# Where the first weight piece of the next stage is loaded and split: eighth chunk or last chunk

## The reference

```python
def swiglu(x, w_gate, w_up, w_down):
    return (jax.nn.silu(x @ w_gate) * (x @ w_up)) @ w_down

# first block
n = modulate(rmsnorm(h, g_pre[l, 0]), shift(0), scale(0))
f = swiglu(n, w_ffn_gate[l, 0], w_ffn_up[l, 0], w_ffn_down[l, 0])
h = h + 0.5 * gate(0) * rmsnorm(f, g_post[l, 0])
...
# a mixer (two attentions) and a second swiglu follow; the second block is alike:
mod = c_act @ ada_w[l] + ada_b[l]
h = modulate_2(rms_norm(x, ffn1_norm[l]), sh1, sc1)
x = x + 0.5 * g1[:, None, :] * swiglu_2(h, ffn1_w_gate[l], ffn1_w_up[l], ffn1_w_down[l])
```

## Time and profile before

| | us |
|---|---|
| median of 3 runs | 1094.05 (1093.93 to 1094.06) |
| the profiled execution's own time | 1094.11 |
| its span | 1092.4 |
| PE busy | 1062.3 (97%) |
| DVE busy | 854.6 (78%) |
| ACT busy | 548.9 (50%) |
| granted TensorE clock | 0.999 |

### The profile page before, as it was taken

How to read it: one execution, slowest core, us unless ns; L and a number is a source line. 1 busy time by engine, 2 the same in 40 slices (tenths; PEclk the granted TensorE clock), 3 DMA queues, 4 the chain that set the end, 5 groups by cost and what they waited for, 6 DMA issues and landing times.

```text
span 1092.4 us, 16231 instructions
## 1 busy us (share of the span) xinstructions
PE 1062.3 (97%) x6159; PEld 927.3 (85%) x6159; DVE 854.6 (78%) x931; ACT 548.9 (50%) x664; POOL 50.3 (5%) x78
## 2 busy tenths in 40 slices
PE   3999999999999999999999999999999999999997
PEld 2999999889988788888978888898887778888886
DVE  6899888678887788887778988877876787666665
ACT  4444343564765654444564444454654456444452
POOL 1000000011121100000010000000100000000001
PEclk9999999999999999999999999999999999999999
DMA  9999997546424599997569999844562536767651
GB/s 342 381 400 391 388 394 261 178 118 221 148 78 154 178 337 312 325 316 234 203 232 343 344 367 342 281 167 135 179 209 100 192 117 212 234 216 233 218 176 58
DMA packets 147141, 265.26 MB, mean 243 GB/s; under 512 B 9770, under 2 KB 104471, under 8 KB 141975
## 3 DMA queue, kind: packets, MB, share of 16 engines
q1 hardware_dynamic: 145376, 261.30, 69.4%
q0 software_dynamic: 1056, 3.17, 0.8%
q10 hardware_dynamic: 662, 0.16, 0.1%
HBM read 263.34 MB, written 1.27 MB: 242 GB/s over the span
## 4 chain that ended last, share of the span: by engine, by line
PE 87%; DVE 4%; DMA 3%; ACT 2%; issue 2%; SPq 1%; POOL 1%; POOLq 0%; DVEq 0%; ACTq 0%
PE ps L1957 18%; PE ps L1888 12%; PE ps L1889 11%; PE ps L1890 11%; PE ps L1963 9%; PE ps L1938 6%; PE ps L1941 6%; PE ps L1940 6%; DMA w_raw<-in_w_ffn_up 1%; ACT w_hi L824 1%; DMA arena<-in_w_ada 1%; DVE w_lo L1209 1%; DVE y_row L1370 1%; PE ps L1908 1%; PE ps L2432 1%
## 5 line engine op out<-in xcount | busy, mean ns | idle before, releaser
L1209 DVE TENSOR_TENSOR w_lo<-w_raw,w_hi 128x2048 fp32r<-128x2048 f32 (+2 forms) x169 | 380.7, 2255 | 104.8 <-ACT w_hi L824 103.8
L824 ACT ACTIVATE w_hi<-w_raw 128x2048 fp32r<-128x2048 f32 (+2 forms) x169 | 317.5, 1883 | 248.8 <-PE ps L1890 93.7
L1957 PE MATMUL ps<-nT_both,w_hi 128*128 128x512 f32 x864 | 210.8, 391 | 0.0
L1957 PEld LDWEIGHTS ps<-nT_both,w_hi 128*128 128x128 f32 x864 | 158.6, 188 | 31.0
L1938 PE MATMUL ps<-nT_both,w_hi 128*128 128x256 f32 x576 | 164.3, 285 | 0.0
L1940 PE MATMUL ps<-nT_both,w_hi 128*128 128x256 f32 x576 | 162.9, 283 | 0.0
L1941 PE MATMUL ps<-nT_both,w_lo 128*128 128x256 f32 x576 | 162.9, 283 | 0.0
L1291 DVE SCALAR_TENSOR_TENSOR arena<-arena,c_act 128x3072 f32<-128x3072 f32 (+2 forms) x49 | 129.4, 2650 | 0.5 <-DMA arena<-in_ada_w 0.5
L1888 PE MATMUL ps<-w_hi,hT_hi 128*128 128x512 f32 x320 | 125.0, 391 | 0.0
L1889 PE MATMUL ps<-w_lo,hT_hi 128*128 128x512 f32 x320 | 125.0, 391 | 0.0
L1890 PE MATMUL ps<-w_hi,hT_lo 128*128 128x512 f32 x320 | 124.5, 389 | 0.0
(11 more groups left out here) (296 smaller groups left out, 1217.7 us busy)
## 6 DMA issues: line engine op xcount, KB each, us to landing
arena<-in_w_ada SPq DMA_DIRECT2D x16, 1536.0 KB, 9.2
arena<-in_ada_w SPq DMA_DIRECT2D x16, 1536.0 KB, 8.5
w_raw<-in_w_in SPq DMA_DIRECT2D x44, 512.0 KB, 4.6
w_raw<-in_ffn_w_down SPq DMA_DIRECT2D x44, 512.0 KB, 4.1
w_raw<-in_w_ffn_gate SPq DMA_DIRECT2D x42, 512.0 KB, 6.7
w_raw<-in_w_ffn_up SPq DMA_DIRECT2D x42, 512.0 KB, 7.7
w_raw<-in_w_ffn_down SPq DMA_DIRECT2D x42, 512.0 KB, 4.6
w_raw<-in_ffn_w_gate SPq DMA_DIRECT2D x42, 512.0 KB, 4.1
```

The source lines that it names most:

```text
L824: copy = lambda o, i: act.activation(o, i, ACT.Copy)
L1209: dve.tensor_tensor(lo(s, n), raw(s, n), hi(s, n).bitcast(F32), ALU.subtract).then_inc(lo_ready[s], 1)
L1957: pe.matmul(ps[:, i, :], hi(s)[:, cols], nT_both[:, 4 * half + k].rearrange("p a n -> p (a n)"), start=(half == 0 and k == 0), stop=False, ...
```

## The change

In F1 and F2 the load of the next stage's E piece moves on SP from behind the down piece of chunk 9 to before `chunk(8)`, that is, behind the B piece of chunk 8 and ahead of the down piece of chunk 7. Its hi split on ACT and its lo split on DVE move from the body of chunk 10 to the body of chunk 8. The loops of the three engines end one chunk earlier, and chunk 8 is written out behind them. F0 and F3 are unchanged, and so is PE's program.

```diff
+        EARLY_NEXT = ("F1", "F2")
...
-                with sp.Fori(3 if f == "F0" else 2, KD + 1) as c:
+                with sp.Fori(3 if f == "F0" else 2, KD if f in EARLY_NEXT else KD + 1) as c:
                     chunk(c)
+                if f in EARLY_NEXT:
+                    next_e()
+                    chunk(KD)
                 load_down(f, NC - 3)
...
                 load_down(f, NC - 2)
-                next_e()
+                if f not in EARLY_NEXT:
+                    next_e()
                 load_down(f, NC - 1)
                 next_b()
...
-                with act.Fori(2, NC - 1) as c:
+                with act.Fori(2, KD if f in EARLY_NEXT else NC - 1) as c:
                     body(f, c)
-                body(f, NC - 1, extra=next_e and (*next_e, n))
+                if f in EARLY_NEXT:
+                    body(f, KD, extra=(*next_e, n))
+                    body(f, NC - 2)
+                body(f, NC - 1, extra=f not in EARLY_NEXT and next_e and (*next_e, n))
...
-                with dve.Fori(3 if f == "F0" else 2, KD + 1) as c:
+                with dve.Fori(3 if f == "F0" else 2, KD if f in EARLY_NEXT else KD + 1) as c:
                     body(f, c, mods=True)
+                if f in EARLY_NEXT:
+                    body(f, KD, mods=True, extra=next_e)
                 body(f, NC - 2, hook=lambda: fold_all(f))
-                body(f, NC - 1, hook=lambda: outs(f), extra=next_e)
+                body(f, NC - 1, hook=lambda: outs(f), extra=None if f in EARLY_NEXT else next_e)
```

## The result

The median is 1096.28 us over 16 runs (1095.54 to 1097.86), against 1094.22 us (1093.85 to 1094.92) for the kernel before in the same measurement. The ratio is 1.0019, with an interval of 1.0012 to 1.0026. The kernel is 2.06 us slower. The forecast was 1096.0 and 2.0 us slower, with a range of 1094.6 to 1097.3.

What follows compares the result with a forecast made beforehand. PE was taken as the bound, busy 1062.3 of 1092.4 us. Removal 0, F1 0 and F2 1.97 us summed to 2.0 us slower, 1096.0 us (ratio 1.0018), with a range of 1094.6 to 1097.3.

Steps and rivals of the forecast that it cites:

- Removal, 0: Last chunks of F1 and F2: taking E's splits out gains 0; bound of the gain is PE's gaps, 1.12 us.
- F1, 0: F1's chunk 8: the product moves by 2.21 us, still ends 0.47 us ahead of PE, so the cost is 0.
- F2, DVE's own share, 0.84: F2's chunk 8: DVE's 2.21 us split moves the product to 701.69, past PE's start at 700.85; PE waits 0.84 us.
- F2, the load's share, 0.98: F2's chunk 8: E's load delays ada half 0, DVE begins 0.98 us late, and all of it reaches the product.
- If ada half 0 lands on time: Sign of a wrong prediction, F2's chunk 8: DVE's ada half 0 was expected to wait about 1 us for its DMA.
- the push of 1.46: F2's chunk 8, DMA queue: the 0.57 MB of E that miss the gap push later loads back 1.46 us.
- the move out of the loop: Loops end a chunk earlier: register and branch work of a few tens of ns moves; cost 0, 0.3 us either way.
- Restart, 0.1: F2, behind PE's wait before chunk 9: 0.1 us, the difference between the 1.87 us wait and the 1.97 us sum.
- (a): Rival, F2's chunk 8: only DVE's work counts, 0.84 us, ada half 0 lands in time; 1094.9 us; chance 0.14.
- (b): Rival, F2's chunk 8: slower, the push is complete and ada half 0 is 2.7 us late; 1097.2 us; chance 0.15.
- (c): Rival: no wait or a small gain, PE's end gaps shrink and F2's reserve suffices; more likely 1094.0 us; chance 0.07.
- (d): Rival: the load waits in SP's queue for slot E, while the splits still move; time as DVE-only or worse; chance 0.02.

Runs made afterwards that it cites:

- after: The kernel with the whole change, in F1 and F2, against the kernel before: 1096.28 us, ratio 1.0019; its profiled execution took 1096.8 us.
- f1_only: The change in F1 alone, F2 as in the kernel before: 1094.59 us, ratio 1.0012; six runs at 1093.98 to 1094.59, five at 1096.34 to 1098.41.
- split_in_chunk9: Kernel before, but in F1 and F2 E is loaded after chunk 8's loads and both its splits are in chunk 9: 1095.48 us, ratio 1.0010.
- f2_small_load: The change in F2 alone, with only 32 of 2048 columns per DMA of E loaded and both splits kept: 1095.85 us, ratio 1.0018.
- before: The kernel without the change, as first profiled: 1094.22 us median in the main measurement; the profiled execution took 1094.11 us.
- f2_only: The change in F2 alone, F1 as in the kernel before: 1096.20 us, ratio 1.0020.
- after_again: The changed kernel measured and profiled once more, nothing altered, against the kernel before: 1095.92 us, ratio 1.0015.
- f2_load_only: Kernel before, but in F2 SP loads E ahead of chunk 8's loads; both splits stay in the last chunk: 1094.37 us, ratio 1.0000.
- before_again: The kernel before, unedited, measured and profiled once more as a kernel of its own: 1094.08 us, ratio 0.9994.
- f2_lo_behind_again: Repeat of the kernel with the change in F2 alone and DVE's lo split of E behind chunk 8's product: 1095.12 us, ratio 1.0009.
- f2_lo_behind: The change in F2 alone, but DVE's lo split of E stands behind chunk 8's product, not ahead of A's split: 1094.66 us, ratio 1.0004.
- f2_lo_one_and_half: The change in F2 alone, with the first 1024 columns of E's lo split done once more in chunk 8: 1098.98 us, ratio 1.0033.

## Why the prediction was right, and where its terms were off

**Removal, 0.** Right. Both ends have the length they had, 38.60 and 25.31 us by the marks above. Of the 1.12 us of gaps named as the bound nothing came.

**F1, 0.** Right in every profile with F1's part. The reserve that was said to remain, 0.47 us, was enough: in after the product ends at 512.13 and PE begins at 512.62. The upper five runs of f1_only stay unexplained. split_in_chunk9 shows that it was worth naming: 0.58 us of wait came up there one chunk later.

**F2, DVE's own share, 0.84.** The mechanism is shown. The 2.2 us pass in full to the product, the wait follows the size of the split (half, one, one and a half, two: 0.49, 1.27, 2.27 and 3.41 us longer chunks), and it goes away when the split goes behind the product. The size was too small, because the reserve of 1.37 us was read from one execution. It wanders by 0.7 us with what DVE waited in chunk 2, and in most executions it is smaller. With ada half 0 at 1.46 us, the median of the eleven that waited for no DMA, it is 1.46 + 16.15 + 0.06 - 16.59 = 1.08 us; f2_small_load measured 1.11.

**F2, the load's share, 0.98.** The place is right, the size was too large. DVE does wait for ada half 0's DMA, as the forecast said, but 0, 0.25, 0.37, 0, 0 and 0.66 us in the six profiles that have both load and a split ahead of the product: 0.2 on the mean. "If ada half 0 lands on time" was one of the prediction's own signs of being wrong, and in half of these profiles, after among them, it did. From issue to landing it took 8.4 to 9.1 us in four executions without the early load, and 9.4 to 10.6 in nine with it (median 10.0), some 1.3 us more, near the push of 1.46. That is partly luck: in f2_small_load, the same program without most of E's bytes, it took 7.9 us. So the bytes pushed by some 2.1 us, and something else in the moved program gave 0.8 back. What that is isn't shown. What failed is the step from the landing to DVE. First, SP issued ada half 0 earlier against PE: 8.38 to 8.95 us before chunk 8 where it had been 7.67 to 8.25. Against PE the landing moved only from 0.76 to 1.29 us, medians. Most of SP's lead of some 0.5 us comes from the move out of the loop, which the forecast had put at a few tens of ns. SP's queue in the kernel after, as in the earlier trace rows:

```profile
675.16 0.82 SPq L571 DMA_DIRECT2D w_raw<-in_ffn_w_down  x2
676.02 2.33 SPq L581 DMA_DIRECT2D arena<-in_ada_w  x2
```

From the down piece's first issue to ada half 0's it takes 0.86 us, as in all ten profiles with F2's chunk 8 outside SP's loop (0.86 or 0.87). In the four with it inside, it takes 1.23 us. That makes 0.37 us. Second, DVE itself is later in most executions than the one of the earlier trace rows, so the room is more than 0.48 us. And more was moved than the 391 GB/s of the sum.

**Restart, 0.1.** This is what lies between 1.87 and 1.97 us in the forecast's sum for F2: what PE loses at its start behind a wait beyond the wait itself. No row of the kernel before gives it. The runs give 0.1 to 0.2: from the start of chunk 9 to M2, PE takes 42.00 to 42.09 us behind a wait, against 41.87 to 41.92 without one. Of this 0.1 is at once: in after the second matmul behind the wait starts 0.34 us after the first, where 0.23 is usual there. The first weight load begins with the first matmul, both at 702.21, while in before it begins 0.22 us ahead of it.

**Sum.** 1.1 + 0.2 + 0.2 = 1.5 us by these terms, and 1.35, 1.45 and 1.69 in the profiles of after, f2_only and after_again. Measured by medians were 2.06, 1.94 and 1.66 us. So the forecast of 2.0 came out right partly by luck: one term was too small and another too large, and something outside F2 adds 0 to 0.7 us. In after's profile it is 0.7 us in M2 (its part up to the out projection is 129.52 us against 128.86, PE waits there 1.8 in place of 1.1), 0.3 us in the last stretch and 0.2 us ahead of F1. after_again has 128.94 in M2.

Whether the change causes the part in M2 is not settled, but the profiles point that way. PE's wait there is 1.1 to 1.4 us in the four whose F2 doesn't load E ahead of chunk 8, and 1.2 to 3.3 us in the ten that do, over 1.5 in eight of them (medians 1.2 and 1.7 us). Against it: f2_load_only has a wait of 1.7 us in its profile and the time of the kernel before.

**Rivals.** (a), DVE's work only, came near as a mechanism: three of six profiles have no DMA wait at all. Its time, 1094.9, was too low by the reserve's spread and the rest outside F2. (b), DVE 2.2 us late behind a full push, is excluded: the longest wait for the DMA is 0.66 us. (c) and (d) are excluded by the 1.0 us of wait and by the split of E at 694.39. The figure weighed in the prediction, some 358 GB/s per core (the Trainium skill, page "DMA: Bandwidth & Descriptors", section Specifications), would have given 2.2 us when the sum is redone, an estimate. The rows after are still further from it, 440 GB/s over 2 us.

**What stays open.** Why the upper times come in 5 of 11 runs of f1_only and in 10 of 22 of the two kernels with lo behind the product, but in 8 of 116 of the kernel before, and whether it is M2's wait each time: of these fifteen runs a single one was profiled, and it is none of f1_only's.

## What to carry to other kernels

A step that is moved to a place where its engine "has room" has to be held against the reserve of the next signal that PE waits for, not against the engine's idle time. In F2's chunk 8 DVE had 1.6 us idle in the window and 1.37 us of reserve, and a step of 2.2 us cost the difference. Read the reserve from several executions before a tenth of a microsecond is made to count, and ask whether a wait in an earlier chunk has moved it. A piece written out behind a loop also changes when its DMAs are issued (0.37 us here). And place the step behind the signal (there it cost nothing in F2), not ahead of it.

## What the runs showed of the hardware

**The clock behind a wait.** From F2's chunk 8 on, behind waits of PE of 2.7, 2.8, 3.2 and 3.3 us the granted clock fell from 2.4 to 1.2 GHz, and the stretch behind took 1.2 to 1.6 us longer than one without the fall. Behind the waits of 2.4, 2.1 and less it stayed. So by the profiles half a split more in F2 cost its own 1.0 us, and a whole one cost 2.1 and 1.6 on top. The kernel's opening is left out: there the windows show 1.00 even behind a wait of 3.0 us (before, at 25.5 us), but matmuls of one form start 0.43 us apart behind it, and 0.23 us apart from 29.2 us on. So the granted clock in the windows does not tell the opening.

**The DMAs of one core moved up to 453 GB/s over 2 us.** With another 1.05 MB waiting, after and f2_load_only moved 418 to 453 GB/s in the windows from 679 to 683 us, in which the kernel before had moved 371 to 379. That the full queue is the cause is not shown: f2_small_load, where that load is 0.03 MB, moved 446 and 406, and before_again 408 and 399. Two windows of f2_load_only, as those of the earlier trace rows:

```profile
675.00:677.00 2.00, 2.00 (x13) 1.78 (x13) 2.00 (x2) 0.64 (x2) 0.00 (x0) 1.00 1.07 391
...
679.00:681.00 2.00, 2.00 (x11) 1.64 (x10) 0.82 (x3) 1.22 (x3) 0.00 (x0) 1.00 1.10 453
```

**One and the same issue differs, and so does its transfer.** From the first of SP's eight DMAs of `w_out` to the end of the last it took 12.45, 13.70 and 13.99 us in before, f2_lo_behind_again and f2_lo_behind, with the same instructions there. In all fourteen profiles PE's wait in M2 is this stretch less 11.3 us (12.45 goes with 1.13, 14.63 in f2_lo_one_and_half with 3.31). The first of the eight alone, before and f2_lo_behind:

```profile
857.58 0.51 SPq L545 DMA_DIRECT2D w_raw<-in_w_out  x1
```

```profile
857.42 1.54 SPq L547 DMA_DIRECT2D w_raw<-in_w_out  x1
```
